# A sparse attention mixer with its compression inside the projection and its heads skewed into the output projection

## The chip, the core and the metric

The kernel runs on one core of a Trainium2 chip. The metric is device time in microseconds (us) of that core, from start to end of the program. TensorE is PE in the profile, its loading of stationary operands PEld, VectorE is DVE, ScalarE is ACT, GpSimd is POOL, and SP issues DMAs.

## The reference, cut to what matters

The program is a chain of transformer blocks over 256 tokens of width 1024. The change lies in one of them, a mixer with native sparse attention and a short convolution, between two feed-forward blocks. Its input is normalised and projected to queries (8 heads of 64), keys and values of two groups, three gates for each head, compression inputs, and three convolution tensors of 512 columns. In short:

```python
# compressed branch: blocks of 32 tokens, stride 16, 15 of them
hidden = gelu(blocks(kv) + pe @ w1); kc, vc = hidden @ w2      # for each group
# three branches for each head, each with its own softmax and mask, ALiBi slope 2**-(h + 1)
s = q @ k.T * d**-0.5 - slope * distance
o = g0 * softmax(s_cmp) @ vc + g1 * softmax(s_slc) @ v_slc + g2 * softmax(s_win) @ v_win
# convolution branch: b, c, x of the projection
conv = c * (causal_conv3(b * x) + bias)
x = x + rmsnorm(concat(o, conv) @ w_out)
```

With 256 tokens the selected and the windowed branch see all causal keys, so the kernel treats both as plain causal attention over 256 keys.

## The kernel before, in words

Activations lie as features by tokens: 8 tiles of 128 features by 256 tokens. Products with weights are done in three matmuls (function `product`, L213 to L218): the high and low parts of weight and activation, in a rounded format, high by high, low by high and high by low. Weights come in chunks of 128x1024 through a ring: SP loads a chunk (L173), ACT rounds it to its high part (L182, `round_high`), DVE subtracts to get the low part (L190, `split_low`), and PE takes it (`arrived`). One chunk makes one tile of output with 24 matmuls of 256 columns.

Each stage is one block: every engine runs its own instruction list, ordered by hand, with semaphores between them, and all engines meet at the end of the block. Every engine goes through its list strictly in order. The mixer (`nsa_mixer`, L2185) is four blocks:

- `nsa_project` (L2203): 24 chunks. The order of outputs is 4 tiles of queries, 4 of compression input, 2 of keys, 2 chunks of values, 12 of convolution input. Before chunk 4, PE does the gates, 32 short matmuls of 24 columns (L2233). DVE copies each output out of PSUM and scales it (L2281 to L2291), then splits the weights of a chunk that lies four ahead.
- `nsa_compress` (L2298): DVE adds the position embedding (L2322) and runs the short convolution (`short_conv`, L2488), PE multiplies the hidden layer (L2337, 32 matmuls of 30 columns, two records each), ACT applies the gelu (L2353), PE makes compressed keys and values.
- `nsa_heads` (L2358): 16 items, a head and one half of the tokens each; 128 keys for the first half and 256 for the second. There are two loops, one after the other. In the first, PE makes scores of the two branches (L2394) and the compressed one (L2396) for all items, DVE adds the bias and takes the maximum (L2436 to L2444), ACT takes the exponentials and sums (L2467). In the second, DVE divides and gates (L2449 to L2459), PE transposes (L2407, L2409), ACT copies the transposes (L2476, L2479), PE multiplies by the values (L2418, L2421), and ACT copies the output (L2484).
- `project_late` (L616) with `SplitOutput` (L494): a few matmuls without use (`keep_warm`, L339), the split of the outputs into high and low parts (L508, L513), and the output projection, whose first three chunks are multiplied tile by tile of the operand (L648 to L654).

A matmul of two f32 operands has two records in the trace (each streams its columns); one in the rounded format and a transpose have one.

## Time and profile before

| what | value |
|---|---|
| device time, median of 3 runs | 2487.01 us (2486.57 to 2493.37) |
| the profiled execution | 2496.24 us, of which the span is 2494.4 us |
| mean granted PE clock | 0.956 of full speed |
| PE busy | 2216.2 us (89%) |
| DVE busy | 1646.4 us (66%) |
| ACT busy | 1007.5 us (40%) |
| instructions | 40984 |

Times in the trace count from the start of the span. In tables by stretch, each engine has its busy time and in brackets its number of instructions, then the granted clock of PE (1.00 is 2.4 GHz, 0.50 is 1.2 GHz), the share of DMA time and GB/s. In a timeline, the columns are start, length, engine, line, operation, operands and count; brackets tell how long the engine sat idle before and who released it. Neighbouring instructions of the same kind are merged into one row, whose length runs from the first start to the last end.

### The profile page before, as it was taken

The page shows a single profiled execution, that of the slowest core. Times are in us where ns is not written, and L with a number is a line of the kernel's source. Part 1 is how long each engine was busy: PE and PEld are TensorE (multiplying, and loading weights), DVE is VectorE, ACT ScalarE, POOL GpSimd, SP SyncE. Part 2 cuts the span into 40 slices and gives each one's busy share as a digit, 9 for nine tenths or more (in the row PEclk, how much of TensorE's full clock was granted, in tenths as well). Part 3 has the DMA queues.
Part 4 walks back from the last instruction along what each step waited for, and adds up shares of the span by engine and source line. Part 5 has one row for each costly group of instructions (what it writes and reads, how often), then busy time and mean ns, then how long its engine had stood idle before and what let it go on. Part 6 is the DMA issues. An engine that isn't in the chain of part 4 may idle for free. (4 is left out here: it accounts for less than half of the span.)

```text
span 2494.4 us, 40984 instructions
## 1 busy us (share of the span) xinstructions
PE 2216.2 (89%) x16088; PEld 1829.5 (73%) x16088; DVE 1646.4 (66%) x3179; ACT 1007.5 (40%) x1955; POOL 540.1 (22%) x549
## 2 busy tenths in 40 slices
PE   8988998867777777778999989999999898999998
PEld 7987988723332333326999977999999877888998
DVE  6676755766666667646667573766766768648666
ACT  5553534523333333334435344434544465014433
POOL 0000001877777777771000000000000000000000
PEclk9999999999998998999999957999999999999999
DMA  5530552799999999993555501455455432002553
GB/s 203 180 111 2 163 176 97 273 410 409 409 409 409 409 409 409 409 409 121 186 185 173 179 24 43 153 181 187 144 186 184 142 105 99 3 3 88 190 186 112
DMA packets 140319, 509.45 MB, mean 204 GB/s; under 512 B 15968, under 2 KB 16608, under 8 KB 139744
## 3 DMA queue, kind: packets, MB, share of 16 engines
q1 hardware_dynamic: 65824, 237.32, 28.7%
q0 software_dynamic: 73728, 268.47, 27.1%
q8 instruction: 129, 2.11, 0.3%
q10 hardware_dynamic: 576, 1.05, 0.1%
q14 instruction: 62, 0.51, 0.1%
HBM read 505.72 MB, written 1.05 MB: 203 GB/s over the span
## 5 line engine op out<-in xcount | busy, mean ns | idle before, releaser
L182 ACT ACTIVATE weights_high<-weights 128x1024 fp32r<-128x1024 f32 x436 | 460.2, 1059 | 526.5 <-PE ps L218 396.1
L216 PE MATMUL ps<-moving_high,weights_high 128*128 128x256 f32 x2224 | 638.7, 287 | 7.8 <-DVE moving_low L833 3.3
L1790 PE MATMUL ps<-v_rows,subkeys 128*128 128x512 f32 x1024 | 490.7, 632 | 171.9 <-ACT subkeys L1844 171.8
L218 PE MATMUL ps<-moving_high,weights_low 128*128 128x256 f32 x2224 | 633.3, 285 | 0.0
L217 PE MATMUL ps<-moving_low,weights_high 128*128 128x256 f32 x2224 | 633.2, 285 | 0.0
L190 DVE TENSOR_TENSOR weights_low<-weights,weights_high 128x1024 fp32r<-128x1024 f32 x419 | 513.6, 1228 | 180.6 <-ACT weights_high L182 177.3
L1790 PEld LDWEIGHTS ps<-v_rows,subkeys 128*128 128x128 f32 x1024 | 198.4, 202 | 463.0 <-issue 463.0
L1950 DVE CUSTOM_DVE_ANT_0 u_rows<-u_rows,ps 128x1024 f32<-128x1024 f32 x256 | 308.9, 1220 | 232.6 <-DMA u_rows<-in_peer_u,experts 232.2
L216 PEld LDWEIGHTS ps<-moving_high,weights_high 128*128 128x128 f32 x2224 | 430.3, 193 | 12.7 <-issue 10.4
L217 PEld LDWEIGHTS ps<-moving_low,weights_high 128*128 128x128 f32 x2224 | 430.0, 193 | 0.5
L218 PEld LDWEIGHTS ps<-moving_high,weights_low 128*128 128x128 f32 x2224 | 429.9, 193 | 0.0
L1856 POOL DMA_INDIRECT u_rows<-in_peer_u,experts x256 | 240.4, 939 | 93.2 <-issue 54.8
L1860 POOL DMA_INDIRECT v_rows<-in_peer_v,experts x256 | 241.6, 944 | 78.1 <-issue 75.1
L3129 POOL COPY inverse_t<-consts 128x512 f32<-128x512 f32 x8 | 4.5, 610 | 983.7 <-POOLq L2585 924.9
L1833 ACT ACTIVATE expert_gelus<-expert_dots,token_scale 128x2 f32<-128x2 f32 x128 | 37.8, 295 | 436.0 <-DVE expert_dots L1950 436.0
L2047 PE MATMUL ps<-hidden_high,weights_high 128*128 128x256 f32 x704 | 200.9, 285 | 5.9 <-DVE hidden_low L2151 5.7
L2047 PE MATMUL ps<-hidden_low,weights_high 128*128 128x256 f32 x704 | 200.4, 285 | 0.0
L2047 PE MATMUL ps<-hidden_high,weights_low 128*128 128x256 f32 x704 | 200.3, 285 | 0.0
L2047 PEld LDWEIGHTS ps<-hidden_high,weights_high 128*128 128x128 f32 x704 | 136.1, 193 | 7.1 <-issue 7.1
L2047 PEld LDWEIGHTS ps<-hidden_low,weights_high 128*128 128x128 f32 x704 | 136.2, 193 | 0.0
L2047 PEld LDWEIGHTS ps<-hidden_high,weights_low 128*128 128x128 f32 x704 | 136.1, 193 | 0.0
L190 POOL TENSOR_TENSOR weights_low<-weights,weights_high 128x1024 fp32r<-128x1024 f32 x17 | 40.5, 2397 | 384.0 <-ACT weights_high L182 383.9
(555 smaller groups left out, 3274.8 us busy)
## 6 DMA issues: line engine op xcount, KB each, us to landing
weights<-in_l_ffn SPq DMA_DIRECT2D x264, 512.0 KB, 4.0
weights<-in_w_in SPq DMA_DIRECT2D x44, 512.0 KB, 3.8
weights<-in_l_in SPq DMA_DIRECT2D x24, 512.0 KB, 3.6
weights<-in_l_rkv SPq DMA_DIRECT2D x24, 512.0 KB, 3.5
weights<-in_w_ckv SPq DMA_DIRECT2D x16, 512.0 KB, 4.3
weights<-in_w_pq SPq DMA_DIRECT2D x16, 512.0 KB, 3.5
weights<-in_w_up_pair SPq DMA_DIRECT2D x8, 512.0 KB, 3.6
weights<-in_w_mix_out SPq DMA_DIRECT2D x8, 512.0 KB, 4.3
```

What stands on the lines that cost most here:

```text
L182: act.activation(self.high[:, c % SPLIT, :], self.raw[:, c % RING, :], ACT.Copy)\
L190: v.tensor_tensor(self.low[:, c % SPLIT, :], self.raw[:, c % RING, :], self.high[:, c % SPLIT, :].bitcast(F32), ALU.subtract).then_inc(sel ...
L216: pe.matmul(out, lhs.high, rhs.high, start=start, stop=False)
L217: pe.matmul(out, lhs.high, rhs.low, start=False, stop=False)
L218: return pe.matmul(out, lhs.low, rhs.high, start=False, stop=stop)
L1790: last = pe.matmul(k.ps[:, 2 * tb + half, :], diagonal[:, i % DIAGONALS, :], v_rows[:, i % V_RING, 512 * half:512 * half + 512], start=i < ...
L1833: act.activation(gelus[:, i:i + 2], dots[:, i:i + 2], ACT.Gelu, scale=k.token_scale[:, block_of(i):block_of(i) + 1]).then_inc(S["gelus"], 1)
L1856: pool.indirect_dma_start(out=u_rows[:, i % U_RING, :], out_offset=None, in_=k.dram["peer_u"], in_offset=index).then_inc(k.u_ready[i % U_R ...
L1860: pool.indirect_dma_start(out=v_rows[:, i % V_RING, :], out_offset=None, in_=k.dram["peer_v"], in_offset=index).then_inc(k.v_ready[i % V_R ...
L1950: v.tensor_tensor_reduce(out=row, in0=row, in1=tokens[block_of(i)], scale=1.0, scalar=0.0, op0=ALU.mult, op1=ALU.add, accum_out=dots[:, i: ...
L2047: last = pe.matmul(acc[:, o, :], w[:, o, :], m, start=f == n == 0 and o % 2 == 0, stop=f == FT - 1 and n == 2, skip_group_check=True)
L3129: pool.tensor_copy(u[:, g, :, :], over(k.const("identity"), 4)).then_inc(S["identities"], 1)
```

## The change

The mixer becomes two blocks. The convolution steps, the block inputs, the hidden layer and the compressed keys and values move into `nsa_project`, whose chunks come in a new order (compression input, convolution input, keys, values, queries). The heads move into the block of the output projection as its `make`. Their 16 items are run in one loop, in which PE has the scores of item i + 2, the transposes of item i and the outputs of item i - 2. The slope goes into the scale of query and exponential, so that one `tensor_tensor_reduce` per branch adds the mask and takes the maximum, and one matmul makes the scores of both branches. The compressed branch is done for all 16 items at once. Outputs of a pair of heads stay in PSUM until ACT and DVE split them into the operand of the projection.

```diff
+NSA_ORDER = [*range(4, 8), *range(12, 24), *range(8, 12), *range(4)]
...
+    misc[:, QUERY_SCALE:QUERY_SCALE + 4] = NSA_DIM ** -0.5 * 2.0 ** (heads + 1)
+    misc[:, SLOPES:SLOPES + NSA_HEADS] = 2.0 ** -(np.arange(NSA_HEADS)[None, :] + 1.0)
...
+class NsaHeads:
...
+    order = (4, 5, 6, 7, 0, 1, 2, 3)
+    roots_first = False
+    AHEAD = BEHIND = 2
...
+        self.items = [(NSA_REP * g + j, tb) for j in range(NSA_REP) for g in range(NSA_GROUPS) for tb in range(TB)]
...
+        def scores(i):
+            h, tb, g, j, keys, half, tok = self.at(i)
+            if i >= 2:
+                pe.wait_ge(S["biased"], i - 1)
+            pe.matmul(k.ps[:, i % 2, 0:2 * keys].rearrange("p (b n) -> p b n", b=2), m["q"][half, j, tok],
+                      m["k_sw"][half, :, 0:keys], start=True, stop=True).then_inc(S["scores_ready"], 1)
+
+        def transposes(i):
+            h, tb, g, j, keys, half, tok = self.at(i)
+            pe.wait_ge(S["probs_ready"], i + 1)
+            if i >= 2:
+                pe.wait_ge(S["transposed_out"], i - 1)
+            for b in range(2):
+                for c in range(tb + 1):
+                    last = pe.transpose(k.ps[:, 4 + i % 2, P * (2 * b + c):P * (2 * b + c) + P],
+                                        self.p[:, i, T * b + P * c:T * b + P * c + P], k.const("identity"))
+            last.then_inc(S["transposed"], 1)
+
+        def outputs(i):
+            h, tb, g, j, keys, half, tok = self.at(i)
+            pe.wait_ge(S["transposed_out"], i + 1)
+            if i == 0:
+                pe.wait_ge(S["cmp_transposed_out"], 1)
+            if j >= 2 and i % 4 == 0:
+                pe.wait_ge(S["parts_ready"], 4 + j - 1)
+            out = k.ps[half, 6 + j % 2, tok]
+            for b in range(2):
+                for c in range(tb + 1):
+                    pe.matmul(out, m["v_sw"][:, c, b, half], p_t[:, i % 4, 2 * b + c, :], start=b == 0 and c == 0,
+                              stop=False)
+            pe.matmul(out, m["vc"][:, j, half], self.c_t[:, NSA_GROUPS * tb + g, :], start=False, stop=True)\
+              .then_inc(S["outputs_ready"], 1)
+
+        keep_warm(k, pe, 4, 7)
+        for i in range(self.AHEAD):
+            scores(i)
+        for tb in range(TB):
+            for j in range(NSA_REP):
+                for g in range(NSA_GROUPS):
+                    half, at = slice(64 * g, 64 * g + 64), 16 * (NSA_REP * tb + j)
+                    pe.matmul(k.ps[:, 2 + g, at:at + N_CMP], m["q"][half, j, P * tb:P * tb + P], m["kc"][half, :],
+                              start=True, stop=True).then_inc(S["cmp_scores_ready"], 1)
+        for i in range(self.N):
+            if i + self.AHEAD < self.N:
+                scores(i + self.AHEAD)
+            transposes(i)
+            if i == self.BEHIND:
+                pe.wait_ge(S["cmp_probs_ready"], 1)
+                for n in range(TB * NSA_GROUPS):
+                    last = pe.transpose(k.ps[:, 2, P * n:P * n + P],
+                                        self.c[:, NSA_REP * n:NSA_REP * n + NSA_REP, :].rearrange("p j n -> p (j n)"),
+                                        k.const("identity"))
+                last.then_inc(S["cmp_transposed"], 1)
+            if i >= self.BEHIND:
+                outputs(i - self.BEHIND)
+        for i in range(self.N - self.BEHIND, self.N):
+            outputs(i)
...
+        def exps(i):
+            h, tb, g, j, keys, half, tok = self.at(i)
+            act.wait_ge(S["max_ready"], i + 1)
+            for b in range(2):
+                part = p[:, i, T * b:T * b + keys]
+                last = act.activation(part, part, ACT.Exp, bias=self.top[:, i, b:b + 1], scale=2.0 ** -(h + 1),
+                                      accum_out=self.total[:, i, b:b + 1])
+            last.then_inc(S["exps_ready"], 1)
+
+        def tile_high(j):
+            act.wait_ge(S["outputs_ready"], 4 * j + 4)
+            act.activation(high[:, j, :], k.ps[:, 6 + j % 2, 0:T], ACT.Copy).then_inc(S["high_ready"], 1)
+
+        for t in range(4, KT):
+            act.activation(high[:, t, :], m["o"][:, t, :], ACT.Copy).then_inc(S["high_ready"], 1)
+        for i in range(self.AHEAD):
+            exps(i)
+        for i in range(self.N):
+            tb = self.at(i)[1]
+            act.wait_ge(S["transposed"], i + 1)
+            if i >= 4:
+                act.wait_ge(S["outputs_ready"], i - 3)
+            act.activation(self.p_t[:, i % 4, :, :].rearrange("p (b c) n -> p b c n", b=2)[:, :, 0:tb + 1, :],
+                           k.ps[:, 4 + i % 2, :].rearrange("p (b c n) -> p b c n", b=2, c=2)[:, :, 0:tb + 1, :],
+                           ACT.Copy).then_inc(S["transposed_out"], 1)
+            if i + self.AHEAD < self.N:
+                exps(i + self.AHEAD)
+            if i == 0:
+                act.wait_ge(S["cmp_shifted"], 1)
+                act.activation(self.compressed(), self.compressed(), ACT.Exp).then_inc(S["cmp_exps"], 1)
+            if i == self.BEHIND:
+                act.wait_ge(S["cmp_transposed"], 1)
+                act.activation(self.c_t[:, :, :].rearrange("p t n -> p (t n)"), k.ps[:, 2, :], ACT.Copy)\
+                   .then_inc(S["cmp_transposed_out"], 1)
+            if i % 4 == 2 and i >= 6:
+                tile_high((i - 6) // 4)
+        tile_high(3)
...
+        def biased(i, b):
+            h, tb, g, j, keys, half, tok = self.at(i)
+            delta = k.consts[:, CONST_ROWS.index("causal0"), :] if tb == 0 else \
+                k.consts[:, CONST_ROWS.index("causal1a"):CONST_ROWS.index("causal1b") + 1, :].rearrange("p a n -> p (a n)")
+            if b == 0:
+                v.wait_ge(S["scores_ready"], i + 1)
+            ins = v.tensor_tensor_reduce(out=p[:, i, T * b:T * b + keys], in0=k.ps[:, i % 2, keys * b:keys * b + keys],
+                                         in1=delta, scale=1.0, scalar=CLAMP, op0=ALU.add, op1=ALU.max,
+                                         accum_out=top[:, i, b:b + 1])
+            if b == 1:
+                ins.then_inc(S["biased"], 1)
+
+        def minus_max(i):
+            v.wait_ge(S["biased"], i + 1)
+            v.tensor_scalar(top[:, i, :], top[:, i, :], CLAMP, -2.0 ** -(self.at(i)[0] + 1), ALU.max, ALU.mult)\
+             .then_inc(S["max_ready"], 1)
...
+        def totals(i):
+            v.wait_ge(S["exps_ready"], i + 1)
+            v.tensor_scalar(total[:, i, :], total[:, i, :], 1e-30, None, ALU.max).then_inc(S["totals"], 1)
+
+        def inverses(i):
+            v.wait_ge(S["totals"], i + 1)
+            v.reciprocal(total[:, i, :], total[:, i, :]).then_inc(S["inverses"], 1)
+
+        def gated(i):
+            h, tb, g, j, keys, half, tok = self.at(i)
+            v.wait_ge(S["inverses"], i + 1)
+            for b in range(2):
+                part = p[:, i, T * b:T * b + keys]
+                last = v.tensor_scalar(part, part, total[:, i, b:b + 1], m["gates"][:, tb, 3 * h + b + 1:3 * h + b + 2],
+                                       ALU.mult, ALU.mult)
+            last.then_inc(S["probs_ready"], 1)
...
+        def compressed_shifted():
+            v.wait_ge(S["cmp_scores_ready"], self.N)
...
+        def tile_low(j):
+            v.wait_ge(S["high_ready"], 4 + j + 1)
+            v.tensor_tensor(parts.low[:, j, :], k.ps[:, 6 + j % 2, 0:T], parts.high[:, j, :].bitcast(F32), ALU.subtract)\
+             .then_inc(S["parts_ready"], 1)
+
+        own.did(v.memset(self.c[:, :, :], 0.0))
+        for i in range(self.AHEAD):
+            biased(i, 0)
+            biased(i, 1)
+            minus_max(i)
+        own.settle()
+        for i in range(self.N):
+            ahead = i + self.AHEAD < self.N
+            totals(i)
+            if ahead:
+                biased(i + self.AHEAD, 0)
+            inverses(i)
+            if ahead:
+                biased(i + self.AHEAD, 1)
+            gated(i)
+            if ahead:
+                minus_max(i + self.AHEAD)
+            if i == 0:
+                compressed_shifted()
+            if i == 1:
+                compressed_gated()
+            if 3 <= i < 7:
+                conv_low(i + 1)
+            if i % 4 == 3 and i >= 7:
+                tile_low((i - 7) // 4)
+        tile_low(3)
...
+                for n, t in enumerate(make.order):
+                    pe.wait_ge(S["parts_ready"], make.ready(n))
                     for i, tiles in enumerate(first_three):
                         last = product(pe, k.ps[:, banks[i], 0:T], tiles[:, t, :], parts[:, t, :],
-                                       start=t == 0, stop=t == KT - 1)
-                        if t == KT - 1:
+                                       start=n == 0, stop=n == KT - 1)
+                        if n == KT - 1:
...
-        nsa_compress(k, m)
-        nsa_heads(k, m)
-        project_late(k, "l0_mix_post_g_2", m["parts"], SplitOutput(k, m["o"], m["parts"]))
+        project_late(k, "l0_mix_post_g_2", m["parts"], NsaHeads(k, ctx, m))
...
+    GATES_BEFORE, CONV, KEYS, VALUES, QUERIES = 4, 4, 16, 18, 20
+    HIDDEN_BEFORE, COMPRESSED_BEFORE = (9, 11), 14
+    TAPS = CMP_STRIDE
...
+                def hidden_layer(kv):
+                    pe.wait_ge(S["blocks_ready"], 4 * kv + 4)
+                    if kv == 0:
+                        pe.wait_ge(S["cmp_loaded"], 32)
+                        pe.wait_ge(S["root_ready"], 1)
+                    else:
+                        pe.wait_ge(S["gates_out"], 1)
+                    for i in range(TAPS):
+                        last = pe.matmul(k.ps[:, 7 - kv, 0:NSA_GROUPS * N_CMP], w1[:, kv, i, :],
+                                         blocks[:, kv, i, :, :].rearrange("p g n -> p (g n)"),
+                                         start=i == 0, stop=i == TAPS - 1)
+                    last.then_inc(S["hidden_ready"], 1)
+
+                def compressed():
+                    pe.wait_ge(S["gelus"], 2)
+                    for g in range(NSA_GROUPS):
+                        pe.matmul(k.ps[64 * g:64 * g + 64, 4 + g, 0:N_CMP], w2[:, 0, :], hidden[:, g, :],
+                                  start=True, stop=True)
+                        for j in range(NSA_REP):
+                            last = pe.matmul(k.ps[:, 7, P * j + 64 * g:P * j + 64 * g + 64],
+                                             shifted[:, g, P * j:P * j + P], w2[:, 1, :], start=True, stop=True)
+                    last.then_inc(S["keys_ready"], 1)
...
+                    if i in HIDDEN_BEFORE:
+                        hidden_layer(HIDDEN_BEFORE.index(i))
+                    if i == COMPRESSED_BEFORE:
+                        compressed()
+                    if VALUES <= i < QUERIES:
+                        if i == VALUES:
+                            pe.wait_ge(S["keys_out"], 1)
...
+                            act.wait_ge(S["shifted_cleared"], 1)
+                            for g in range(NSA_GROUPS):
+                                last = act.activation(
+                                    shifted[:, g, :].rearrange("p (j n) -> p j n", j=NSA_REP)[:, :, 0:N_CMP],
+                                    over(k.ps[:, 6, N_CMP * g:N_CMP * g + N_CMP], NSA_REP), ACT.Gelu_apprx_tanh)
+                            last.then_inc(S["gelus"], 1)
+                            act.activation(table_load[:, :], k.const("ones")[:, 0:1], ACT.Exp)
...
+                    if CONV <= i < CONV + 4:
+                        if i == CONV:
+                            v.wait_ge(S["pos_loaded"], 16)
+                            v.wait_ge(S["copied"], CONV)
+                        block_tokens((i - CONV) // 2, (i - CONV) % 2)
+                    if i == COMPRESSED_BEFORE:
+                        v.wait_ge(S["keys_ready"], 1)
+                        for g in range(NSA_GROUPS):
+                            half = slice(64 * g, 64 * g + 64)
+                            v.tensor_copy(m["kc"][half, :], k.ps[half, 4 + g, 0:N_CMP])
+                        v.tensor_copy(m["vc"][:, :, :].rearrange("p j n -> p (j n)"), k.ps[:, 7, :])\
+                         .then_inc(S["keys_out"], 1)
+                    if i == KEYS:
+                        v.wait_ge(S["copied"], KEYS)
+                    if KEYS <= i:
+                        short_conv(k, v, own, m, z, i - KEYS)
...
```

The short convolution is the same work in five steps, one after each of the chunks 16 to 20. The block inputs (8 additions), the copies of compressed keys and values and the scaling of the queries are kept.

## Rows read from the trace of the kernel before

**Rows 1.** page, part 2: busy tenths and granted clock in 40 slices

```profile
PE   8988998867777777778999989999999898999998
PEclk9999999999998998999999957999999999999999
```

**Rows 2.** busy time by stretch; columns: stretch, length, engines, clock, DMA

```profile
1380.00:1439.00 59.00, 56.09 (x466) 55.89 (x464) 33.04 (x40) 22.94 (x23) 0.00 (x0) 0.98 0.53 171
1439.00:1458.00 19.00, 15.23 (x72) 14.57 (x72) 12.28 (x26) 1.68 (x3) 0.00 (x0) 0.52 0.09 28
1458.00:1486.00 28.00, 26.66 (x96) 23.69 (x96) 21.05 (x76) 19.24 (x90) 0.00 (x0) 0.50 0.00 1
1486.00:1528.50 42.50, 39.67 (x152) 26.02 (x152) 18.78 (x101) 13.09 (x46) 0.00 (x0) 0.50 0.00 1
1528.70:1534.50 5.80, 5.76 (x40) 3.89 (x40) 0.00 (x0) 2.81 (x10) 0.00 (x0) 1.00 0.01 3
```

**Rows 3.** timeline, first and last rows of the four blocks' borders

```profile
1435.82 0.28 PE L218 MATMUL ps<-moving_high,weights_low 128*128 128x256 f32 x1
1439.36 4.63 DVE L2322 TENSOR_TENSOR cmp_blocks<-cmp_in,cmp_pos 64x240 f32<-64x240 f32 x8 [0.85 <-PEq L2214]
...
1537.44 0.36 PE L216 MATMUL ps<-moving_high,weights_high 128*128 128x256 f32 x1 [0.84 <-DVE moving_low L513]
```

**Rows 4.** timeline of PE, the gates and the next chunk, then the hidden layer

```profile
1372.32 4.38 PE L2233 MATMUL ps<-w_g,x_residual 128*128 128x24 f32 x32
1376.52 0.56 PE L216 MATMUL ps<-moving_high,weights_high 128*128 128x256 f32 x1
...
1441.71 13.86 PE L2337 MATMUL ps<-cmp_blocks,cmp_w 128*128 128x30 f32 x64 [5.62 <-DVE cmp_blocks L2322]
```

**Rows 5.** busy time by stretch, around the gates

```profile
1371.60:1375.00 3.40, 3.40 (x33) 3.40 (x32) 3.40 (x6) 1.44 (x2) 0.00 (x0) 1.00 0.51 169
1376.50:1381.60 5.10, 5.10 (x25) 5.10 (x26) 0.00 (x0) 0.00 (x0) 0.00 (x0) 0.50 0.58 207
1382.00:1384.80 2.80, 2.80 (x26) 2.80 (x26) 1.65 (x2) 2.69 (x4) 0.00 (x0) 1.00 0.00 0
```

**Rows 6.** timeline of DVE, one chunk of the projection

```profile
1416.20 0.42 DVE L2287 TENSOR_TENSOR conv_in<-ps,inverse_rms 128x256 f32<-128x256 f32 x1 [0.47 <-PE ps L218]
1417.35 1.23 DVE L190 TENSOR_TENSOR weights_low<-weights,weights_high 128x1024 fp32r<-128x1024 f32 x1 [0.73 <-ACT weights_high L182]
1419.05 0.42 DVE L2287 TENSOR_TENSOR conv_in<-ps,inverse_rms 128x256 f32<-128x256 f32 x1 [0.47 <-PE ps L218]
```

**Rows 7.** costliest groups between 1439 and 1545 us, one of DVE

```profile
L2322 DVE TENSOR_TENSOR cmp_blocks<-cmp_in,cmp_pos 64x240 f32<-64x240 f32 x8 | 4.4, 552 | 1.1 <-PEq L2214 0.9
```

**Rows 8.** timeline of PE in the heads, at the lower clock

```profile
1459.49 2.05 PE L2394 MATMUL ps<-nsa_k,nsa_q 64*128 64x256 f32 x4
...
1489.70 1.12 PE L2407 MATMUL ps<-consts,nsa_probs 128*128 128x128 f32 x4 [0.31 <-DVE nsa_probs L2459]
1494.07 1.97 PE L2421 MATMUL ps<-nsa_probs_t,nsa_v 128*64 128x128 f32 x8
1495.97 1.12 PE L2407 MATMUL ps<-consts,nsa_probs 128*128 128x128 f32 x4
```

**Rows 9.** timeline of PE in the heads, at the higher clock

```profile
1530.36 1.09 PE L2421 MATMUL ps<-nsa_probs_t,nsa_v 128*64 128x128 f32 x8
```

**Rows 10.** timeline of DVE, a tensor_tensor_reduce, then reciprocal and gating of one item

```profile
1370.06 0.28 DVE L2273 CUSTOM_DVE_ANT_0 inverse_rms<-inverse_rms,consts 128x128 f32<-128x128 f32 x1
1370.39 0.42 DVE L2281 SCALAR_TENSOR_TENSOR nsa_q<-ps,inverse_rms 128x256 f32<-128x256 f32 x1
...
1488.48 0.18 DVE L2451 RECIPROCAL nsa_sum<-nsa_sum 128x3 f32<-128x3 f32 x1
1488.89 0.62 DVE L2457 TENSOR_SCALAR nsa_probs<-nsa_probs,nsa_sum 128x256 f32<-128x256 f32 x2
```

**Rows 11.** busy time by stretch, in the delta rule of the first mixer

```profile
228.00:234.00 6.00, 3.65 (x30) 3.24 (x28) 0.00 (x0) 2.66 (x5) 0.00 (x0) 1.00 0.00 0
```

More of the change, by code:

```diff
@@ L66 @@
 HEAD_SELECT = 64
+QUERY_SCALE, SLOPES = 96, 100
 EPS_AT = {1: 48, 4: 49, 640: 50}
@@ L517 @@
 class RwkvNorm:
+    order = range(KT)
+    roots_first = True
     def __init__(self, k, ctx, m, parts):
@@ L631, in _ @@
             def _(act):
-                act.activation(table_load[:, :], k.const("ones")[:, 0:1], ACT.Sqrt)
+                if make.roots_first:
+                    act.activation(table_load[:, :], k.const("ones")[:, 0:1], ACT.Sqrt)
                 make.scalar(act, S)
+                if not make.roots_first:
+                    act.activation(table_load[:, :], k.const("ones")[:, 0:1], ACT.Sqrt)
                 k.w.round_high(act, first)
```

326 lines of the change are left out of this document (114 added, 212 removed).

## Prediction

> **What bounds the kernel now.** I read the busy slices of the page first. PE is busy 89% of the span, and the granted clock stands at 9 tenths nearly everywhere; only two slices beside each other show 5 and 7 tenths [rows 1]. They are this mixer. The table by stretch splits it [rows 2]: in the projection PE works at 0.98 of full speed for 56.09 of 59 us; in the compression (1439 to 1458) and in both loops of the heads (1458 to 1528.5) it is granted 0.50, the lower of its two levels, 1.2 GHz. It is busy nearly all of that time, at half the pace. Only from 1528.7 on the same kind of work has 1.00. So three things are to be weighed: work that leaves the stretch between the projections, waits inside it, and the clock in it.
>
> The stretch that the change rewrites runs from the last matmul of the projection, 1435.82 (end 1436.10), to the first of the output projection, 1537.44 [rows 3]: 101.3 us. The meeting of all engines at the first border takes until about 1439.3 [rows 3] and stays, so 98.2 us are at stake, called the middle.
>
> **The projection, which takes in the compression.** PE is the bound here: a chunk takes 2.85 us of PE, and DVE sits waiting for PE in each (0.42 of copy and 1.23 of split out of 2.85) [rows 6]. What PE gets is therefore added in full; what DVE and ACT get is hidden.
> - PE gets two hidden layers of 32 records and the compressed keys and values, 20 records (8 matmuls for the values instead of 2, since four shifted copies are made). The nearest row is the gates' burst: 32 short records in 4.20 us, from 1372.32 to 1376.52 [rows 4]. With the clock lost at about 1375.0 [rows 5] that is 2.7 us for 24 of them, 0.112 each at full clock, and twice that at half (64 of the hidden layer in 13.86 us, 0.214 each) [rows 4]. 84 records by 0.112 make 9.4 us.
> - The gates' burst also cost the clock: the chunk behind it ran at 0.50 until about 1381.6 [rows 5], where 5.1 us held 25 matmuls against 26 in 2.8 us at 1.00. So a burst can cost 2.5 us behind it and up to 1 us in it. A hidden layer is a shorter burst (3.6 us at full clock). Bounds: no such fall, 9.4 us; one for each layer, 16. I take a little less than half a fall for the two together, **+10.8 us**.
> - DVE gets 8 additions of 0.55 us [rows 7], two for each of four chunks: 1.65 + 1.10 of 2.85, just fits. The convolution steps come after chunks 16 to 20. All that DVE did in the compression block is 12.28 us [rows 2], against 1.2 us of slack in each of 24 chunks (29 us); PE is three copies behind at most, and a lag of a few us is made up before chunk 23. ACT gets two more table loads and is busy 22.94 of 59 us [rows 2]. New chunk order and same DMAs on SP: nothing. All of this is hidden, cost 0; if the cover went (a DVE lag at the end) it would be some 2 us.
>
> **The middle: one loop for the heads.** The engines go through their lists in order, so I follow the loop around. In round i PE has scores(i+2), transposes(i), outputs(i-2). DVE has totals(i), biased(i+2), inverses(i), gated(i). DVE's gated(i+1) comes behind biased(i+3), which waits for scores(i+3), which on PE stand behind transposes(i) and outputs(i-2), and transposes(i) wait for gated(i). So the round is serial: what PE does in one round and what DVE does from biased to gated lie one behind the other. Only totals, minus_max, the exponentials, the copies of ACT and the low parts lie beside it.
> - PE's leg. An f32 record of 128 columns takes 0.213 us at half clock (eight in 1.97, the last ending 0.42 after its start, with the gap behind the first) [rows 8] and 0.109 at full (eight in 1.09) [rows 9]. One of 256 columns takes 0.427 at half [rows 8]. For 128 keys: 2 transposes and 6 records of outputs; for 256 keys 4 and 10. The scores have 2 records of 256 or 512 columns, 0.85 or 1.71 us. On average 11 short records and 1.28 us: 3.63 at half, 1.86 at full. Every change of group adds some: a pair of items before takes 6.27 us (1489.70 to 1495.97) for 24 records of 0.213, in six groups [rows 8], so 0.19 for a group, 0.15 at full (my estimate). With three groups, 0.2 until the result is in and two handoffs of 0.05: 4.5 at half, 2.6 at full.
> - DVE's leg. A tensor_tensor_reduce of 128 columns holds the engine for 0.33 with its accumulator read (1370.06 to 1370.39) [rows 10]; for 256 columns 0.13 more. The reciprocal 0.2, the gating of 256 keys 0.62 [rows 10], of 128 some 0.15 less. Average of both sizes: 2 x 0.40 + 0.2 + 0.55 = 1.5 us.
> - A round: **6.0 us at half clock, 4.1 at full**. Before, an item took 28/16 = 1.75 us in the first loop and 3.14 in the second [rows 2, 8], 4.9 together, at half clock, since the loops had no such chain. The skew makes a serial round out of two streams.
> - 13 rounds hold scores: 78 or 53 us. Ahead of the first: keep_warm 1.7, scores(0) and (1) 2.6 or 1.3, the compressed scores of all items 32 short records, 6.8 or 3.6, scores(2), DVE's leg and group starts 2.7: 13.8 or 8.9. Behind the last: 52 short records and 8 groups, 12.9 or 7.1. The compressed branch makes one long wait in round 2 (4 transposes, exponentials, a copy), some 1 us, and the first two rounds have no outputs: together -1 or +1.
> - The end of the middle: the output projection follows in the same block, tiles 4 to 7 are ready by then and cover the last split. That removes 3 us of border and is in the sum.
> - Sum: **103.7 us at half clock, 70 at full**, against 98.2.
>
> **Which clock.** None of the rows shows this loop. The new start has what took the clock before: 3 us of idle PE at the border, then 3.6 us of records with 15 columns, shorter than the gates' 24, at whose burst the clock fell [rows 5]. I take it as lost there. In the rounds PE then waits 1.6 of 6 us for DVE, while before it was at 0.50 through 42.5 us with 39.67 busy [rows 2]. That speaks for half all through. Against it: the records of scores and outputs stand closer together than before, and the same kind of work did rise to 1.00 at 1528.7 [rows 2]. I take full clock for about a quarter of the middle: 103.7 - 0.23 x 33.7 = **96 us**, and keep both ends.
>
> The Trainium skill, "TensorE: Matmul & The Clock Gate", section "HAM oscillation — how this bites in real kernels", says that waits between bursts of matmuls bring the clock down again and again. By it the middle takes all 103.7 us. The trace is not of one mind with it: in the delta rule PE is busy 3.65 of 6 us and keeps 1.00 [rows 11], and in the heads it is busy nearly throughout and stays at 0.50 [rows 2].
>
> **Sum of the forecast.** Middle 96 - 98.2 = -2.2, projection +10.8: **+8.6 us**, taken as +8. The profiled execution took 2496.24 us, 9.2 above the median of 2487.01 and 1.8 above its span; it should come to 2504. Against the median: **2495 us**. This kernel's measurement can tell about 0.3%, 7.5 us, from no change, so the forecast sits on that line.
>
> **Rivals.**
> 1. *The clock stays low all through.* 103.7 and 10.8 to 13: +16 to +18, 2504 us. For it: rows 2; against it: the rise at 1528.7. Chance 0.25.
> 2. *The clock stays high, and it is faster.* If the 4 keep_warm matmuls and the closer records hold 1.00, the middle takes 70 us, the projection 9.4: -19, 2468 us. It decides at the compressed scores: with a fall of only one short stretch there and 1.00 in the rounds the result is already under the old time. From 40% of the middle at full clock on, the sum turns negative. Rows 11 speak for it, rows 5 against. By the page's rule it can't be. Chance 0.18, with all results under -7.5.
> 3. *The loop is not serial in the way I read it*, because DVE finds its scores ready. Then PE alone is the bound, 3.63 + 0.57 a round at half, 67 + 27 = 90 to 94 us with start and end, and with +10.8 it comes to 2490. Nothing in the lists shows how. Chance 0.12.
> 4. *The projection pays more*: a fall at both layers and a late split, 16 + 2, on top of the forecast, 2503. Chance 0.05.
> The forecast itself, middle 88 to 101 us: 0.40.
>
> **How the numbers follow.** The likeliest case gives 2495, its own range is 2487 to 2501. The range goes down to 2473, where the clock is high for two thirds of the middle, and up to 2506, rival 1 with the dearer projection; rival 2 at its full size is left out. Faster by over 0.3%: rival 2 and a little, 0.22. Within 0.3%: half of the forecast and rival 3, 0.30. Slower: the rest, 0.48.
>
> **What would show it.** In the profile of the changed kernel: rounds of scores, 6 us apart where the granted clock is 0.50 and 4 us where it is 1.00; DVE idle in the rounds, released by the scores on PE, and PE idle, released by the gating; the projection 10 to 13 us longer by its own short records; the copies of outputs there still waiting for PE. I am wrong if the rounds are shorter than 5 us at 0.50, if DVE's waits are for ACT, or if the clock is at 1.00 through the rounds.

## The result, and the profile after

| | before | after |
|---|---|---|
| median, same chip | 2487.01 us (17 runs, 2481.03 to 2506.24) | 2498.86 us (17 runs, 2488.57 to 2504.0) |
| ratio | | 1.0042, 95% interval 1.0028 to 1.0056 |
| the profiled execution | 2496.24 us | 2502.79 us, span 2500.7 |

The change costs 0.4%, some 10 us of the median; the forecast was 2495 us, +8. All ratios leave out two disturbed executions on one chip, 3545.01 us of scores_early and 3059.54 us of before.

The trace after does not seem to say so at first. All "mixer" times here run from 7.5 us behind the first projection matmul of the mixer (equal in all profiles) to the first matmul of the output projection; "projection" ends with the start of the last product of three, "middle" is the rest. In the shown pair the mixer went from 172.5 to 168.1 us (projection 70.7 to 82.0, middle 101.9 to 86.2): 4.4 us **shorter**, where the median is 10 us longer. In the pair of profiled executions the rest of the program, whose code was not touched, went from 2321.9 to 2332.6 us. So either the change costs outside the mixer, or one of the two profiles is not typical; the experiments settle that first.

Part 2 of the page after, busy tenths of PE and its granted clock in 40 slices, to lay beside [rows 1]:

```profile
PE   8988998877777877778999978999999898999998
PEclk9999999999999989999999977999999999999999
```

The two slices in which the clock is low have 7 and 7 tenths where before they had 5 and 7. The table by stretch after (columns as in [rows 2]) has, row by row, the projection, keep_warm, the compressed scores, the rounds and the tail:

```profile
1369.90:1452.30 82.40, 82.40 (x654) 81.80 (x652) 54.17 (x87) 29.55 (x33) 0.00 (x0) 0.94 0.47 145
1455.60:1459.00 3.40, 3.40 (x8) 2.48 (x8) 0.48 (x1) 1.30 (x4) 0.00 (x0) 0.50 0.52 164
1459.00:1462.40 3.40, 3.40 (x38) 2.82 (x38) 1.71 (x11) 1.52 (x7) 0.00 (x0) 1.00 0.00 0
1462.40:1529.00 66.60, 47.33 (x156) 26.86 (x155) 24.28 (x141) 19.33 (x71) 0.00 (x0) 0.60 0.00 0
1529.00:1538.00 9.00, 7.97 (x52) 6.49 (x52) 3.38 (x14) 2.83 (x8) 0.00 (x0) 0.72 0.00 0
```

PE still has no gap in the projection. In the rounds it is busy 47.33 of 66.60 us, where before it was busy nearly throughout [rows 2]. The waits after, from 1459 to 1541 us (engine, tile and line, who ended the wait, us in total, times, the longest):

```profile
ACT nsa_probs_t L621 <- PE ps L551: 51.3, 16, 6.4
DVE nsa_probs L649 <- PE ps L541: 46.3, 15, 6.0
PEld ps L551 <- DVE nsa_probs L673: 33.1, 14, 3.2
PE ps L551 <- DVE nsa_probs L673: 19.3, 14, 1.6
```

L541 is the scores, L649 the biased scores with their maximum, L673 the gating, L551 the transposes: DVE waits for PE and PE for DVE, about once in each item. The timeline of PE and DVE in one round, where both legs lie end to end:

```profile
1495.96 1.55 PE L541 MATMUL ps<-nsa_k,nsa_q 64*128 64x512 f32 x2
1497.55 0.43 DVE L649 CUSTOM_DVE_ANT_0 nsa_probs<-ps,consts 128x256 f32<-128x256 f32 x1 [2.33 <-PE ps L541]
...
1497.98 0.40 DVE L649 CUSTOM_DVE_ANT_0 nsa_probs<-ps,consts 128x256 f32<-128x256 f32 x1
...
1498.31 0.73 DVE L673 TENSOR_SCALAR nsa_probs<-nsa_probs,nsa_sum,nsa_gates 128x256 f32<-128x256 f32 x2
...
1499.10 1.11 PE L551 MATMUL ps<-consts,nsa_probs 128*128 128x128 f32 x4 [1.58 <-DVE nsa_probs L673]
...
1500.14 1.97 PE L565 MATMUL ps<-nsa_probs_t,nsa_v 128*64 128x128 f32 x8
...
1502.46 0.79 PE L541 MATMUL ps<-nsa_k,nsa_q 64*128 64x256 f32 x1
```

From one set of scores to the next it is 6.5 us for this item of 256 keys; DVE's leg is 1.55 of them (1497.55 to 1499.10), and PE stands idle through it.

### The profile page after: what moved, and what is told of

It reads as the page before. It is cut to its first block and busy times, and to the rows that moved or that the text cites. A ratio compares the mean times of both kernels' runs of the same rounds, so it can differ in the third digit from the quotient of the medians.

```text
span 2500.7 us, 40828 instructions
## 1 busy us (share of the span) xinstructions
PE 2214.9 (89%) x16058; PEld 1819.6 (73%) x16058; DVE 1634.6 (65%) x3163; ACT 996.6 (40%) x1895; POOL 541.5 (22%) x549
## 5 line engine op out<-in xcount | busy, mean ns | idle before, releaser
L221 PEld LDWEIGHTS ps<-moving_high,weights_high 128*128 128x128 f32 x2224 | 430.6, 194 | 12.8 <-issue 10.4
```

The lines of the kernel that those rows point to most:

```text
L221: pe.matmul(out, lhs.high, rhs.high, start=start, stop=False)
```

## Experiments

Profiles of all kernels, one each, in us; "at half" is the time at a granted clock of 0.50 in the mixer. Ratios are to before on the same chip. before_again, after_again, projection_alone and heads_alone ran on a chip where before takes 2561.51 us, all others on chips where it takes 2487 to 2491 us.

| kernel | mixer | projection | middle | at half | ratio (95%) |
|---|---|---|---|---|---|
| before, first profile | 172.5 | 70.7 | 101.9 | 95.6 | |
| before_again | 172.7 | 70.8 | 101.9 | 95.6 | 1.0006 (0.9986 to 1.0026) |
| before_third | 158.4 | 67.6 | 90.8 | 64.9 | 1.0005 (0.9967 to 1.0042) |
| constants_only | 159.8 | 69.1 | 90.7 | 68.3 | 0.9994 (0.9973 to 1.0015) |
| inert_instructions | 158.3 | 67.6 | 90.7 | 64.9 | 0.9998 (0.9984 to 1.0012) |
| after, first profile | 168.1 | 82.0 | 86.2 | 71.7 | 1.0042 (1.0028 to 1.0056) |
| after_again | 166.4 | 80.3 | 86.1 | 68.3 | 1.0032 (1.0014 to 1.005) |
| projection_alone | 158.2 | 82.0 | 76.2 | 68.3 | 0.999 (0.9974 to 1.0007) |
| heads_alone | 180.9 | 67.6 | 113.4 | 95.6 | 1.008 (1.0053 to 1.0107) |
| scores_early | 137.7 | 82.0 | 55.7 | 30.7 | 0.9912 (0.9889 to 0.9936) |
| gated_first | 142.6 | 80.4 | 62.3 | 41.0 | 0.991 (0.9885 to 0.9934) |
| spread_hidden | 132.9 | 77.2 | 55.7 | 20.5 | 0.9911 (0.988 to 0.9942) |
| warm_border | 136.7 | 81.9 | 54.8 | 27.3 | 0.9917 (0.9886 to 0.9949) |
| all_edits | 134.4 | 77.2 | 57.2 | 23.9 | 0.9899 (0.9866 to 0.9932) |

**before_again**, no edit.

> The kernel before, once more. In the first pair of profiles the mixer (first projection matmul to first output-projection matmul) went from 172.5 to 168.1 us, and all the rest of the program from 2321.9 to 2332.5 us, with 126 and 168 us at half clock in it. Theory A (the medians differ by what the change does in the mixer, and the first profiles had an unlike mixer clock): a second profile of before has a mixer clearly under that of after, 160 to 165 us, and the same rest as after. Theory B (the mixer is as in the first profile, 172 to 173 us in every execution, and the difference lies elsewhere in the program): mixer 172 to 173 us, rest 2315 to 2322 us. Ratio 1.000 by both.

**after_again**, no edit.

> The changed kernel, once more. Theory A (the change costs in the mixer, the first profile was a lucky one): mixer 173 to 180 us, since the share of full clock in the rounds changes between executions; rest near 2325 us. Theory B (the cost lies outside the mixer, in the clock of stages whose code was not touched): mixer 166 to 170 us again, rest over 2328 us again. Ratio 1.003 to 1.006 by both.

Both mixers came out as theory B has them, and on this chip the whole program took 2561.51 us instead of 2487. But both profiled executions of before lay 8 to 9 us above their medians (2569.14 against 2561.05 here), those of after 4 above and 1 below. Theory B is not shown by this: both profiles of before could be untypical.

**projection_alone**: the changed projection, with the heads, the query scale and the split of before. The diff is cut to the calls.

```diff
-        project_late(k, "l0_mix_post_g_2", m["parts"], NsaHeads(k, ctx, m))
+        nsa_heads(k, m)
+        project_late(k, "l0_mix_post_g_2", m["parts"], SplitOutput(k, m["o"], m["parts"]))
```

> The projection part alone: compression in the projection, the two loops of the heads and the split as before. By the forecast's own terms the projection is 10.8 us longer and the compression block with its border (22 us, 1436.1 to 1458.0 less nothing kept but one border) goes: mixer 172.5 + 10.8 - 22 + 3 = 164 us, about 8 us under before, with the heads unchanged at 79 us from their first scores to the output projection. Rival: the compression costs the same inside the projection as outside (16 or more, since each short burst brings the clock down and the chunks behind it run at half): mixer 170 us or more.

**heads_alone**: projection and compression block of before (with the shifted copies of the values that the new heads read), and the new heads. The diff is cut to the calls.

```diff
         nsa_project(k, m)
+        nsa_compress(k, m)
         project_late(k, "l0_mix_post_g_2", m["parts"], NsaHeads(k, ctx, m))
```

> The heads part alone: projection and compression block as before, the 16 items in one loop in the block of the output projection. The serial loop (transposes wait for gating, gating for the scores three items on) gives rounds of about 5 us as in the first profile of the changed kernel and 82 us from the first scores to the output projection, against 79 with a border: mixer 172 to 176 us, no gain from the heads. Rival (the skewed loop hides latency and is what saved the 15.7 us of the middle): 10 us or more faster than before, mixer 162 us or less.

The mixers were 158.2 and 180.9 us, outside both expectations, one lower and one higher. Against the 172.5 us of before the medians make no sense: projection_alone would be 14 us faster, and measured 3 (with an interval of 4 to both sides). Against some 159 us they do: -1 and +22, measured -3 and +21. All variants agreed on one offset, so the next question was whether it lay in something that they share. The new heads themselves took 82.4 us from their first scores to the output projection, as expected (82); the expected mixer was missed ahead of them, where 31.0 us lie between the last product of the projection and the first scores, against 22.6 in before.

**constants_only** and **inert_instructions**, each on the kernel before:

```diff
+    heads = 4 * (s // 64) + np.arange(4)[None, :]
+    misc[:, 96:100] = NSA_DIM ** -0.5 * 2.0 ** (heads + 1)
+    misc[:, 100:100 + NSA_HEADS] = 2.0 ** -(np.arange(NSA_HEADS)[None, :] + 1.0)
```

> Kernel before, with the twelve constant columns of the change (query scales and slopes) added to the table and not used. All three variants measured so far (the change, its projection part alone, its heads part alone) have a median that is 12 to 13 us longer than before's plus the difference of their mixers (2401.2 to 2402.0 us outside the mixer by median less the profile's mixer, against 2388.8 for before). These columns are the only thing all three share. If the offset comes from them: ratio 1.004 to 1.006. If not (it comes with any other instruction stream, or is chance): 1.000, within 0.2%; mixer 172.6 us by both.

```diff
                     k.w.round_high(act, first + i + 1)
+                    if 5 < i < NSA_CHUNKS - 1:
+                        for n in range(4):
+                            act.activation(spare[:, 4 * i + n:4 * i + n + 1], k.const("ones")[:, 0:1], ACT.Copy)
```

> Kernel before, with 68 ScalarE copies of one column into a spare tile, four behind each rounding of chunks 6 to 22 in the mixer's projection, where ScalarE is busy 22.94 of 59 us. The work beside it hides them: mixer 172.6 us, within 1 us. If any change of the instruction stream moves the rest of the program by what the three variants showed, the ratio is 1.003 to 1.006 with an unchanged mixer; if the offset is bound to something else, 1.000, within 0.2%.

Neither moved the time, and both profiles showed a mixer of 158 to 160 us. The mixer's work is that of before, so before itself seemed to have two courses. A third profile of the unchanged kernel was the test.

**before_third**, no edit.

> The kernel before, unchanged, a third profile. Its mixer took 172.5 and 172.7 us in two profiled executions that were 8 to 9 us above their medians, and 159.8 and 158.3 us in the two near-copies (constants only, inert instructions) whose medians are the same as before's. Theory (the mixer of before has two courses of the clock, half speed after the border for 88.7 or for 64.9 us, and the shorter one is the common one): 158 to 160 us with 64.9 us at half speed, in an execution near its median, or again 172.5 in one that is 8 us above it. Rival (before's own program always takes 172.5 us there): 172.5 us in an execution near or below the median.

158.4 us, in an execution at 2491.14, 4 us above its median. Its table by stretch (columns as in [rows 2]):

```profile
1436.90:1440.30 3.40, 0.59 (x5) 0.38 (x4) 1.81 (x3) 1.06 (x1) 0.00 (x0) 1.00 0.49 165
1440.30:1505.10 64.80, 56.76 (x225) 47.95 (x226) 49.47 (x189) 26.85 (x115) 0.00 (x0) 0.50 0.03 9
1505.10:1527.80 22.70, 21.25 (x143) 14.49 (x142) 3.19 (x17) 12.66 (x40) 0.00 (x0) 1.00 0.01 1
```

and the same two stretches in the first profile of before:

```profile
1439.90:1504.80 64.90, 57.87 (x229) 48.76 (x230) 49.95 (x194) 26.91 (x116) 0.00 (x0) 0.50 0.02 8
1504.80:1528.60 23.80, 23.80 (x94) 15.56 (x92) 1.62 (x9) 6.51 (x22) 0.00 (x0) 0.50 0.00 0
```

Up to 65 us behind the border both do the same at half speed. Then the clock comes back in the one and stays low for 23.8 us more in the other; in 22.7 us at full speed PE does 143 records, in 23.8 us at half 94. PE's idle time in the middle is 12.3 us in both; the busy time is 89.6 us in the long course and 78.5 in the short one. One of three profiles of before and both of its near-copies have the short course, and the medians of all variants fit it (the sum, below). The first profile, on which the prediction rests, showed the long one. What decides between the two is not known. The distance from the median tells it only in part: both long courses lay 8 to 9 us above it, but constants_only lay 6.6 us above it with the short one.

The rest of the program moves as well: on the chips with 2487 to 2491 us, span less mixer was 2321.9 us in the first profile of before and 2326.9 to 2334.6 in all others, though its code is the same in every kernel. So in the first pair the long course of before hid 14 us of the cost, and its short rest gave 5 to 13 us back.

**scores_early**, on the changed kernel:

```diff
+        scores(self.AHEAD)
         for i in range(self.N):
-            if i + self.AHEAD < self.N:
-                scores(i + self.AHEAD)
+            if i + self.AHEAD + 1 < self.N:
+                scores(i + self.AHEAD + 1)
             transposes(i)
```

> Changed kernel with one edit: PE issues the scores of item i + 3 ahead of the transposes of item i, where they wait only for the bank that biased(i + 1) frees. Theory (the round is serial: the gating releases the transposes, and the scores behind them release the next round on DVE): the loop is broken, DVE finds its scores ready, PE becomes the bound: rounds of 4.2 us at half clock or 2.7 at full instead of 5.05, 13 rounds give back 12 to 30 us, mixer 166.4 to 168.1 before the edit, 138 to 155 after it; DVE's waits for scores go, and the time of the whole falls by 0.5 to 1.2% against the changed kernel. Rival (PE's clock sets the pace and its waits fall in anyway): mixer within 3 us of 167.

**gated_first**, on the changed kernel:

```diff
             totals(i)
-            if ahead:
-                biased(i + self.AHEAD, 0)
             inverses(i)
-            if ahead:
-                biased(i + self.AHEAD, 1)
             gated(i)
             if ahead:
+                biased(i + self.AHEAD, 0)
+                biased(i + self.AHEAD, 1)
                 minus_max(i + self.AHEAD)
```

> Changed kernel with the other end of the same loop cut: DVE does totals, inverses and gated of item i first and the two biased of item i + 2 behind it; PE's order as in the change. Theory of the serial round: gated(i + 1) no longer stands behind biased(i + 3), so PE's transposes find their operand earlier; the loop that is left is biased(i + 2), maximum, exponentials, totals(i + 2), two rounds long, so it should gain nearly as much as the other cut: mixer 140 to 157 us. Rival (it is the late scores alone, or the latency from totals over the reciprocal to the gating, that sets the round): mixer 163 us or more.

137.7 and 142.6 us, as the theory of the serial round has them: the same work, cut at either end of the loop, gives back 24 to 30 us, and both are 0.9% faster than before. The waits of scores_early from 1457.9 to 1506.3 us:

```profile
DVE nsa_probs L650 <- PE ps L541: 12.0, 9, 3.7
...
PE ps L551 <- DVE nsa_probs L674: 2.2, 3, 1.4
```

46.3 us of waiting became 12.0, and 19.3 became 2.2. Its timeline of PE, one pair of items at full clock:

```profile
1478.23 1.12 PE L541 MATMUL ps<-nsa_k,nsa_q 64*128 64x512 f32 x2
1479.29 0.44 PE L551 MATMUL ps<-consts,nsa_probs 128*128 128x128 f32 x2
1479.66 0.65 PE L565 MATMUL ps<-nsa_probs_t,nsa_v 128*64 128x128 f32 x4
1480.14 0.38 PE L567 MATMUL ps<-nsa_cmp_t,vc 128*64 128x128 f32 x2
1480.46 0.70 PE L541 MATMUL ps<-nsa_k,nsa_q 64*128 64x256 f32 x2
1481.08 0.66 PE L551 MATMUL ps<-consts,nsa_probs 128*128 128x128 f32 x4
1481.67 1.09 PE L565 MATMUL ps<-nsa_probs_t,nsa_v 128*64 128x128 f32 x8
1482.59 0.38 PE L567 MATMUL ps<-nsa_cmp_t,vc 128*64 128x128 f32 x2
1482.90 1.12 PE L541 MATMUL ps<-nsa_k,nsa_q 64*128 64x512 f32 x2
```

PE has no wait left; two items take 4.67 us. A part of the gain is the clock, which comes back at 1478.2, 27 us behind the last product of the projection, and then stays. The two profiles separate the parts: the middle has 258 records of PE in both, its idle time goes from 23.5 to 6.4 us and its busy time from 62.7 to 49.3, with 20.5 us at half clock instead of 61.4. So of the 30.5 us some 17 are waits and 13 are the same records done faster. Why the clock stays with shorter waits was not tested by itself.

**spread_hidden**, on scores_early:

```diff
-                    if i in HIDDEN_BEFORE:
-                        hidden_layer(HIDDEN_BEFORE.index(i))
+                    if HIDDEN_AT[0] <= i < HIDDEN_AT[0] + 4:
+                        hidden_chunk(i)
+                        continue
```

where `hidden_chunk` puts one matmul of the hidden layer behind each `product` of chunks 9 to 12. The gelu of each layer and the compressed keys and values come one or two chunks later than before.

> The kernel with early scores (mixer 137.7 us, its projection 82.0), with one edit in the projection: the 32 matmuls of the two hidden layers are not two bursts but stand one behind each three matmuls of chunks 9 to 12. Theory (a hidden layer costs its records, 32 x 0.109 us, and one fall of the clock behind it, 3.4 us at half speed, which is 1.7 us): the records stay, the two falls go, projection 78 to 79 us, mixer 134 to 135. Rival 1 (short records cost the same wherever they stand, and the falls at about 31 and 41 us into the mixer come anyway): projection 81.5 to 82.5. Rival 2 (switching between shapes costs more than the fall): projection 83 us or more.

77.2 us for the projection, from 82.0, and a little under the expected 78 to 79. Its timeline of PE in such a chunk:

```profile
1406.24 0.30 PE L2490 MATMUL ps<-cmp_blocks,cmp_w 128*128 128x30 f32 x2
1406.38 0.36 PE L221 MATMUL ps<-moving_high,weights_high 128*128 128x256 f32 x1
1406.58 0.27 PE L222 MATMUL ps<-moving_low,weights_high 128*128 128x256 f32 x1
1406.70 0.28 PE L223 MATMUL ps<-moving_high,weights_low 128*128 128x256 f32 x1
1406.81 0.30 PE L2490 MATMUL ps<-cmp_blocks,cmp_w 128*128 128x30 f32 x2
```

A product with its pair of short records takes 0.57 us; three matmuls alone take 0.36 (2.85 us for 24). So the records cost the same 0.21 for two as in a burst (0.22), and only the falls are gone; the one at the gates, which comes in some profiles and not in others, was absent here too, worth 1.7 of the 4.8 us (82.0 against 80.3 in the two profiles after). all_edits, the other kernel with the layers spread, has no half clock in its projection either; the six profiles with the layers in bursts have 3.4 to 6.8 us of it behind them. In the whole time (0.9911 against 0.9912) these 5 us are not to be seen, with intervals of 0.3% to both sides.

**warm_border**, on scores_early:

```diff
                     feature_tiles(k, pe, ring(i) % 4, m["parts"], k.w.arrived(pe))
+                keep_warm(k, pe, 8, 7)
```

> The kernel with early scores, with 8 matmuls without use at the end of PE's list in the projection block, where PE otherwise sits idle for 3.2 us until all engines have met. Theory (the half clock at the start of the heads comes from this idle time and then from the waits of the first items, 3.4 and 17.1 us of it in the run before): the first fall goes or shrinks, keep_warm of the next block takes 1.8 us instead of 3.6, middle 55.6 before the edit, 50 to 54 after it. Rival (the fall comes from the thin start of the heads, 32 records of 15 columns and the wait for the first gating, whatever stands before the border): middle 55 to 56 us. If the matmuls reach past the other engines' last work, the middle grows by up to 1 us.

Its table by stretch:

```profile
1446.30:1456.10 9.80, 9.50 (x66) 7.50 (x64) 4.18 (x17) 4.36 (x13) 0.00 (x0) 1.00 0.37 126
1456.20:1473.30 17.10, 14.25 (x42) 7.99 (x40) 10.55 (x58) 6.33 (x22) 0.00 (x0) 0.50 0.00 0
```

The fall at the border is gone (clock 1.00 up to 1456.1), the one in the first items came as before, and the middle got 0.9 us shorter. keep_warm of the next block took 1.8 us instead of 3.6, as expected, but the border before it grew by 0.5 us, and from the first scores on it took 0.3 us more (48.7 for 48.4). In the whole time nothing is seen (0.9917 against 0.9912).

**all_edits**: scores_early, gated_first, spread_hidden and warm_border together.

> Early scores, gating ahead of the biases on DVE, hidden layers spread, and the matmuls at the end of the projection block, together. If the terms are independent: projection 78 to 79, middle 50 to 55, mixer 130 to 134 us, against 172.5 or about 159 of before and 166 to 168 of the change, ratio to before 0.988 to 0.991. If both cuts of the loop do the same thing, the second adds nothing to the first (mixer 133 to 135); if gating ahead of the biases delays the maxima and with them the exponentials two rounds later, it costs 1 to 3 us instead.

Middle 57.2 against 54.8 with the early scores and the warm border alone: the second cut adds nothing and costs 2.4 us, in a stretch at half clock that is 23.9 us long instead of 17.1. That is one profile of each, and whether the clock or the order of DVE comes first was not tried. All five versions with the loop cut are some 20 to 25 us under before and 30 under the change; their ratios (0.9899 to 0.9917, intervals of 0.2 to 0.3% to both sides) do not tell them apart.

## Why the prediction was right, and where it was not

- **The sum** (+8): right in sign and size, in part by luck (the middle, below). Typical mixers are about 159 us before and 167 after, +8; the two measured ratios make +10.4 and +8.2. The same base fits each variant: mixers of 158.2, 180.9, 137.7, 142.6 and 132.9 make -1, +22, -21, -16 and -26, measured -3, +21, -22, -22 and -22, with intervals of 4 to 8 us. Of after and of each variant there are one or two profiles, so that none of them has a second course is not shown.
- **The projection** (+10.8, bounds 9.4 and 16): +12.7 or +12.9 like for like (80.3 against 67.6 without a fall at the gates, and 82.0 against 69.1 with a short one). PE after:

```profile
1396.66 3.65 PE L2480 MATMUL ps<-cmp_blocks,cmp_w 128*128 128x30 f32 x32
1400.15 0.37 PE L221 MATMUL ps<-moving_high,weights_high 128*128 128x256 f32 x1
...
1407.45 3.65 PE L2480 MATMUL ps<-cmp_blocks,cmp_w 128*128 128x30 f32 x32
...
1421.26 0.29 PE L2488 MATMUL ps<-cmp_hidden,cmp_w 128*64 128x15 f32 x2
1421.48 1.10 PE L2491 MATMUL ps<-cmp_w,cmp_hidden_shifted 128*128 128x64 f32 x8
```

  A layer is 3.49 us (0.109 a record, 0.112 forecast), the compressed keys and values 2.4 (1421.26 to 1423.64), together 9.4, which is the lower bound. And 48 matmuls from 1400.15 to 1407.45 take 7.3 us instead of 5.7, and the 72 from 1410.95 to 1421.26 take 10.3 instead of 8.55: 1.6 and 1.8 for a fall behind each layer. The term mis-sized is "a little less than half a fall for the two together" (1.4 us); it was two whole ones, 3.4. Not every layer has its fall: in projection_alone, gated_first and warm_border only the second has. DVE and ACT were hidden, as forecast.
- **The round** (6.0 at 0.50, 4.1 at 1.00): the serial chain is as read, and the two cuts show it. From the gating at 1508.02 to that at 1519.53, all at half clock, two rounds take 11.51 us, 5.76 each. The forecast holds within 5%. Over all, 13 rounds took 65.6 us (1463.63 to 1529.24), 5.05 each. No round ran at full clock from end to end, so the 4.1 was not measured by itself.
- **The start and the tail** (13.8 or 8.9, and 12.9 or 7.1): 8.0 and 8.8 us. The 32 records of 15 columns took 2.3 us at full clock, 0.073 each; "32 short records, 6.8 or 3.6" was too dear. "I take it as lost there" was half right: the clock was at 0.50 in keep_warm ahead of them, at 1.00 in them, and fell again at 1462.4, right behind them.
- **The middle** (96 us and 3.3 of border): 86.2. This is the step that failed in absolute terms, with its base. "98.2 us are at stake" came from an execution in which before stood at half clock for 23.8 us longer than in before_third and both near-copies; the typical middle is 90.7 with its border. Both sides were read 11 to 13 us too long, and the difference of -2.2 came to -4.6. That the errors cancelled was luck, twice over: in the middle, and between the middle (2.4 us too high) and the projection (2 us too low). A warning stood in the prediction itself: the profiled execution lay 9.2 us above the median, which was only subtracted.
- **Which clock**: neither low all through nor high, but up and down. The table by stretch after:

```profile
1462.40:1482.80 20.40, 13.92 (x40) 7.51 (x39) 9.38 (x51) 6.78 (x24) 0.00 (x0) 0.50 0.00 0
1482.90:1486.20 3.30, 2.12 (x12) 1.33 (x12) 1.57 (x10) 0.90 (x4) 0.00 (x0) 1.00 0.00 0
1486.30:1493.00 6.70, 5.12 (x17) 2.94 (x16) 1.97 (x10) 1.72 (x7) 0.00 (x0) 0.50 0.00 1
1493.20:1496.40 3.20, 2.02 (x11) 1.14 (x11) 1.57 (x10) 1.13 (x6) 0.00 (x0) 1.00 0.00 0
1496.60:1503.30 6.70, 5.12 (x18) 3.21 (x16) 1.97 (x10) 1.66 (x6) 0.00 (x0) 0.50 0.00 0
```

  PE is busy 68 to 76% of the slow stretches and 63 to 64% of the fast ones, and the clock changes between them over and over. From keep_warm to the output projection (82.4 us) 61.4 us are at half, so the quarter at full clock is what was taken. The Trainium skill, "TensorE: Matmul & The Clock Gate", section "HAM oscillation — how this bites in real kernels", says that waits between bursts bring the clock down again and again. The trace agrees, with five falls from 1462.4 to 1527.3 us and a rise between each and the next. That the clock stays down all through (103.7 us) and that a high one "can't be" was the prediction's own inference, and not what the section says.
- **The rivals**: a clock low all through (2504 us) and a high one (2468) fell with this table; a loop that is not serial (2490) fell with the waits. Rival 4 was right in its first half, a fall at both layers. Three of these sums do not follow from the prediction's own terms. Rival 3 counts 16 rounds of 4.2 us beside a start and a tail that belong to 13; with 13 it is 55 + 27 us and about 2481 us. The sum turns negative from 48% of the middle at full clock on, not 40%. And 2473 us need nine tenths at full clock; two thirds make 2481. So the lower bound of the range lay deeper than its reason.
- **The two halves of the change**: by projection_alone, compression in the projection is worth nothing (middle -14.5, projection +12.9 to +14.4). The new heads beside it cost 10 us of middle (86.2 against 76.2; alone they and their extra compressed values cost 22.7, 113.4 against 90.7, so the halves do not simply add), in spite of less work: PE is busy 62.7 us instead of 68.4 and idle 23.5 instead of 7.8, and the time at half clock is nearly the same (61.4 and 58.0).

## What to carry to other kernels

Follow each engine's list once around the loop before two streams are skewed into one: if A's next step stands behind a step that waits for B, and B's behind one that waits for A, the round is the sum of both legs, and one line moved on either engine (here the scores one item earlier) breaks it. Before the stretches of one profile are used as a base, take a second and a third and compare the clock stretch by stretch: here the same stretch was 11 us longer in two of three. A profiled execution some us off its median is a reason to ask, though not a proof. Short matmuls cost PE their own time wherever they stand (here 0.21 us a pair of records); spread among long ones they did not bring the clock down behind them, where a burst of 32 records did, for 1.6 to 1.8 us.

## What the runs showed of the hardware

- The same code has two courses of the clock, of 158.4 and 172.5 us in this mixer. The three long stretches of plain products behind it repeat: 1530 matmuls from first to last start in 184.8, 184.8 and 184.6 us, within 0.02 us in all 14 profiles. The one ahead of it (1512 matmuls) does not, with 187.1 to 188.2 us.
- The work of the first 1350 us was not changed, yet on one of the chips the whole took 2561.51 us instead of 2487. 66 us of it lie in the stage that gathers expert rows (451.3 to 1138.7 us in before, 454.5 to 1207.9 in before_again). Its table from 500 to 800 us, first before, then before_again:

```profile
500.00:800.00 300.00, 223.68 (x467) 90.67 (x466) 202.15 (x490) 99.02 (x318) 222.51 (x237) 0.94 1.03 409
```

```profile
500.00:800.00 300.00, 208.81 (x418) 85.77 (x416) 179.85 (x443) 89.07 (x288) 196.84 (x210) 0.86 0.95 365
```

  In the same 300 us PE did 418 records instead of 467, at 0.86 instead of 0.94 and with 365 instead of 409 GB/s. Which of clock and transfers follows the other stays open, and so does whether the chip itself or something beside it on the machine makes the difference.
- The ratios held across the two chips (1.0042 and 1.0032), though the times differ by 3%.
